# Gelu weights per eight picks instead of sixteen, and the weighted sum five steps behind the dots instead of nine

## The chip, the cores and the metric

One core of a Trainium2 chip runs the whole program. The metric is device time in microseconds (us) of one execution; of several executions the median is taken. The trace comes from one profiled execution of the same program.

## The reference, cut to what matters

A hybrid layer is computed for 1024 prompt rows and 64 sample rows: RMSNorm, a projection, a gated delta rule on 4 heads, a forgetting attention on 8 heads, an output projection, then the expert layer that this change touches, then a gated projection and a final norm. The expert layer, per row `t` with 8 heads of 16 picks (128 picks per row):

```python
e    = i1 * N_KEYS + i2                       # 128 expert numbers per row
gate = softmax(cv)                            # over the 16 picks of a head
a    = einsum('thk,td->thk' over d, take(u_tab, e), x)     # one dot of 1024 per pick
wgt  = gate * gelu(a)
y    = einsum('thk,thkd->td', wgt, take(v_tab, e))         # weighted sum of 128 rows of 1024
```

Gelu and the product with the gate act on each pick alone, so they can be taken for any set of picks whose dots are done.

## The kernel before, in words

The work is cut into tiles of 128 rows, and `build` writes one **pass** (`body`) after another, with a barrier of all engines between them: pass 0 has only the front part of tile 0 (norms, projections, both mixers, the choice of the picks); passes 1 to 7 run the front of tile i together with the expert layer of tile i-1 (from pass 2 on also the tail of tile i-2); the sample pass runs the front of the 64 sample rows with the expert layer of tile 7; the folded pass has the expert layer of the sample rows (64 picks for 128 half-rows) and a tail; the last has only a tail.

Inside a pass the order is a list of **slots** (`PLAN`, written by `make_plan`). Each slot names parts of the front and tail; every engine walks through the slots in order and does its share of these parts. After the parts of a slot come the expert steps of the slot (`Schedule`): two u steps (gather 128 rows of `peer_u`, 512 KB, and one dot per row on VectorE, line 1409) and two v steps (gather 128 rows of `peer_v` and add them, weighted, to the sum). A v step is done either on VectorE (line 1417, `scalar_tensor_tensor`) or on TensorE (line 1011, with a 128x128 diagonal matrix that ScalarE makes of the weights, line 731); `on_tensor` decides it by the slot.

The v steps of a slot belong to picks whose u steps stood `LAG` = 9 slots earlier. So slots 0 to 8 have u steps only, slots 9 to 63 both, slots 64 to 72 v steps only; 73 slots in all. When the 16 picks of a head have their dots (8 slots), ScalarE takes their gelu at the start of slot 8, 16, ... (line 736, after the diagonals of that slot and ahead of the slot's parts) and VectorE multiplies it with the gate (line 1401, behind the slot's parts); the signals are `w_gelu` and `w_ready`.

All gathers are issued by GpSimd (line 486) in the order of the steps into a ring of 8 buffers: gather n waits until step n-8 has been used (`consumed`). The first three u gathers of a pass (`AHEAD`) are issued at the end of the pass before, when the new expert numbers are there (`gate_done`, set by the last of the six `pick_gate` parts, in slot 68, lines 1375 and 1378); that pass waits for their landing. GpSimd also does one product of `pick_gate` (line 505) in slot 67, in its own order between the gathers. The weights of the projections come in pieces of 1 MB through a ring of 3 buffers on SyncE's queue (line 264).

Of the kernel before, what the change touches and what calls it, by code (L numbers as in the profile page):

```python
# [8 lines left out]
ACT = mybir.ActivationFunctionType  # L9
# [18 lines left out]
HP, KEYS, TOP = 8, 128, 16  # L28
EXPERTS = KEYS * KEYS
PICKS = HP * TOP  # L30
# [8 lines left out]
AHEAD = 3  # L39
DIAGS = 4  # L40
PER_SLOT = 2
HEAD_SLOTS = TOP // PER_SLOT
LAG = HEAD_SLOTS + 1


TAIL_PIECES = {f"gate{j}": ("gate", 256 * j, 256) for j in range(4)}
# [26 lines left out]
def on_tensor(k):  # L73

    slot = k // PER_SLOT + LAG
    if 23 <= slot < 43:
# [8 lines left out]
class Schedule:  # L85

    def __init__(self, picks, on_tensor):
        self.picks = picks
        self.slots = picks // PER_SLOT + LAG
        self.order = []  # L90
        for s in range(self.slots):
            own = []
            for j in range(PER_SLOT):
                if s < self.slots - LAG:
                    own.append(("u", PER_SLOT * s + j))
                if s >= LAG:
                    own.append(("v", PER_SLOT * (s - LAG) + j))
            self.order.append(own)
# [12 lines left out]
def build(nc, t, out):  # L111
    ctx = ExitStack()
    with ctx:
        def sb(name, shape, dt=F32):
            return ctx.enter_context(nc.sbuf_tensor(name, shape, dt))
# [109 lines left out]
        dots = sb("dots", [P, PICKS])  # L225
        wgt = sb("wgt", [P, PICKS])
# [8 lines left out]
        S = dict(zip(names, sems))  # L235
# [126 lines left out]
        def body(front=None, peer=None, tail=None, blocks=TILES, plan=None,  # L362
# [33 lines left out]
            def wait_landed(eng, n):  # L396

                before = 1 if n % RING < AHEAD else 0
                if n >= AHEAD:
                    eng.wait_ge(landed[n % RING], 16 * (n // RING + 1 - before))  # L400

            def wait_used(eng, kind, k):

                n = sched.number[kind, k]
                eng.wait_ge(consumed[n % RING], n // RING + 1)
# [14 lines left out]
            with nc.Block() as block:  # L420
# [117 lines left out]
                def _(act):  # L538
# [184 lines left out]
                    for s in range(len(plan)):  # L723
                        if peer:
                            for k in [k for kind, k in sched.order[s] if kind == "v" and k in sched.tensor]:

                                m = sched.tensor[k]
                                act.wait_ge(S["w_ready"], k // TOP + 1)
                                if m >= DIAGS:
                                    wait_used(act, "v", sched.tensor_picks[m - DIAGS])  # L730
                                act.activation(diag[0:peer, m % DIAGS, 0:peer], ident[0:peer, 0:peer], ACT.Copy,  # L731
                                               scale=wgt[0:peer, k:k + 1]).then_inc(S["diag_ready"], 1)
                            if s and s % HEAD_SLOTS == 0 and s // HEAD_SLOTS <= sched.picks // TOP:
                                h = s // HEAD_SLOTS - 1
                                wait_used(act, "u", TOP * h + TOP - 1)
                                act.activation(wgt[0:peer, TOP * h:TOP * h + TOP],  # L736
                                               dots[0:peer, TOP * h:TOP * h + TOP], ACT.Gelu)\
                                    .then_inc(S["w_gelu"], 1)
                        for name in plan[s]:
                            next_part(name)  # L740
# [285 lines left out]
                def _(v):  # L1026
# [365 lines left out]
                    for s in range(len(plan)):  # L1392
                        for name in plan[s]:
                            next_part(name)
                        if not peer:
                            continue
                        if s and s % HEAD_SLOTS == 0 and s // HEAD_SLOTS <= sched.picks // TOP:
                            h = s // HEAD_SLOTS - 1
                            v.wait_ge(S["w_gelu"], h + 1)
                            c = slice(TOP * h, TOP * h + TOP)  # L1400
                            v.tensor_tensor(wgt[0:peer, c], wgt[0:peer, c], gate_c[0:peer, c], ALU.mult)\
                                .then_inc(S["w_ready"], 1)
                        for kind, k in sched.order[s]:
                            n = sched.number[kind, k]
                            r = n % RING
                            row = ring[0:peer, r, :]
                            if kind == "u":
                                wait_landed(v, n)
                                v.tensor_tensor_reduce(out=row, in0=row, in1=xn_c[0:peer, :], scale=1.0, scalar=0.0,  # L1409
                                                       op0=ALU.mult, op1=ALU.add, accum_out=dots[0:peer, k:k + 1])\  # L1410
                                    .then_inc(consumed[r], 1)
                            elif k not in sched.tensor:
                                wait_landed(v, n)
                                v.wait_ge(S["w_ready"], k // TOP + 1)
                                if last_add is not None:
                                    wait_used(v, *last_add)
                                v.scalar_tensor_tensor(out=h_c[0:peer, :], in0=row, scalar=wgt[0:peer, k:k + 1],  # L1417
                                                       in1=h_c[0:peer, :], op0=ALU.mult, op1=ALU.add)\
                                    .then_inc(consumed[r], 1)
                                last_add = (kind, k)  # L1420
                    if peer:
# [4 lines left out]
                        for g in range(2):  # L1426
                            c = slice(512 * g, 512 * g + 512)
# [57 lines left out]
def make_plan():  # L1485

    plan = [[] for _ in range(FULL.slots)]

    def at(slot, *names):
        plan[slot].extend(names)  # L1490

    def spread(name, *slots):
        for s in slots:
            at(s, name)

    spread("tail_norm", 0, 1, 2)
    spread("norm_mix", 0, 1, 2)
    spread("fox_past", 3, 4, 5)
    for j in range(6):
        at(3 + j, f"conv_in{j}")  # L1500
    for g in range(3):
        spread(f"conv{g}", 5 + 2 * g, 6 + 2 * g, 7 + 2 * g)
    at(9, "ba_g")
    at(10, "fox_v1")
    spread("gates", 11, 12)
    for j in range(4):
        at(11 + j, f"gate{j}")
    spread("gdn", 12, 13, 14, 15, 16)
    at(15, "proj0")
    at(16, "proj0", "proj1", "fox_v0")  # L1510
    at(17, "proj1", "fox_k0")
    spread("tail_fin", 18, 19, 20)
    at(18, "fox_k1")
    at(19, "fox_q0")
    at(20, "fox_q1")
    spread("fox_keys", 20, 21)
    at(21, "g")
    at(22, "silu_g")
    s = 22
    spread("inv0", s, s + 1)  # L1520
    for l in range(1, LEVELS):
        spread(f"inv{l}", s + 2 * l - 1, s + 2 * l, s + 2 * l + 1)
    s += 2 * LEVELS
    spread("state", s, s + 2, s + 3, s + 4, s + 5)
    spread("gdn_norm", s + 6, s + 7)
    start = [21 + (9 * h + 2) // 4 for h in range(HB)] + [99]
    for h in range(HB):
        s = start[h]
        spread(f"fox_s{h}", *([s] if s != start[h - 1] + 2 else []), s + 1)
        at(s + 2, f"fox_o{h}")  # L1530
        if start[h + 1] == s + 2:
            at(s + 2, f"fox_s{h + 1}")
        spread(f"fox_o{h}", s + 2, s + 3)
    spread("fox_norm", s + 5, s + 6)
    spread("mix_turn", s + 7, s + 8)
    s += 9
    for j in range(4):
        spread(f"out{j}", s + (2 * j) // 3, s + (2 * j) // 3 + 1)
    s += 3
    spread("norm_ffn", s, s + 1, s + 2, s + 3)  # L1540
    s += 3
    for j in range(HP):
        at(s + j, f"wq{j}")
        if j % 2:
            at(s + j, f"scores{j // 2}")
            at(s + j + 1, f"halves{j - 1}")
            at(s + j + 2, f"halves{j}")
            at(s + j + 3, f"pairs{j // 2}")
    s += HP + 3
    spread("pick_gate", s, s + 1, s + 2, s + 3, s + 4, s + 5)  # L1550
    at(HP * HEAD_SLOTS + 1, "hand_rows")
    assert s + 5 < FULL.slots, s
    return plan


PLAN = make_plan()
FIRST_PLAN = first_plan()

# [35 lines left out]
```

## Time and profile before

| what | value |
|---|---|
| median of 3 runs | 4310.57 us (4282.62 to 4318.11) |
| the profiled execution | 4289.45 us |
| its span, first to last instruction | 4287.7 us |
| outside the span | 1.75 us |
| VectorE busy | 3298.2 us (77%) |
| GpSimd busy | 2583.1 us (60%) |
| TensorE matmul busy | 2891.3 us (67%) |
| ScalarE busy | 813.3 us (19%) |
| gathers (GpSimd's queue) | 1140.99 MB of 1454.12 MB |

Busy times are averages over stages with different limits: inside a pass the DMA engines, GpSimd's issuing and VectorE take turns. Passes 1 to 7 and the sample pass take about 450 to 510 us each, the folded pass 204 us. A window below is a stretch of the span in us; DMA share is the mean busy share of the 16 DMA engines (it can read slightly above 1), GB/s what they moved.

### The profile page before, as it was taken

To read this page: it belongs to the slowest core of one execution; us is meant where nothing else is said; L and a number is where in the kernel's file an instruction comes from. 1 tells how busy PE (TensorE), PEld (TensorE's weight loads), DVE (VectorE), ACT (ScalarE), POOL (GpSimd) and SP (SyncE) were. 2 spreads that over 40 slices of the span, in tenths; PEclk is the share of its full clock that TensorE was granted. 3 is DMA by queue.
4 is the path that set the end of the run, shared out by engine and by line. 5 is a ranking of instruction groups with operands and counts; after the bars stand their busy time and mean duration, and the time that the engine had idled before them with its cause. 6 is when DMAs were issued, how large, how long until landed. Compare 5 with 4: busy or idle time off the path is not lost. (4 is left out here: it accounts for less than half of the span.)

```text
span 4287.7 us, 39164 instructions
## 1 busy us (share of the span) xinstructions
PE 2891.3 (67%) x12714; PEld 1950.3 (45%) x12714; DVE 3298.2 (77%) x6492; ACT 813.3 (19%) x1609; POOL 2583.1 (60%) x2285
## 2 busy tenths in 40 slices
PE   6747665865777666867677577776688565766456
PEld 5634443543455344544355345544455334535122
DVE  3477978787977888697878897788868785787764
ACT  2112111211122112221122112211222112211111
POOL 0037766576656756576656666675666654675674
PEclk9868788987889788988799788988798787868677
DMA  5259998999899998999899989999898989999896
GB/s 185 93 223 372 356 385 303 413 357 370 338 375 370 356 382 317 397 360 379 305 412 355 364 337 370 374 342 392 314 405 309 365 320 277 386 349 362 275 387 238
DMA packets 388058, 1454.12 MB, mean 339 GB/s; under 512 B 64528, under 2 KB 67536, under 8 KB 353296
## 3 DMA queue, kind: packets, MB, share of 16 engines
q0 software_dynamic: 313344, 1140.99, 71.3%
q1 hardware_dynamic: 73200, 305.92, 18.4%
q10 hardware_dynamic: 1312, 4.72, 0.3%
q8 instruction: 103, 1.69, 0.2%
q14 instruction: 99, 0.81, 0.1%
HBM read 1441.69 MB, written 9.51 MB: 338 GB/s over the span
## 5 line engine op out<-in xcount | busy, mean ns | idle before, releaser
L486 POOL DMA_INDIRECT ring<-peer_u,idx_c x1061 | 1267.6, 1195 | 782.4 <-DVE dots L1409 402.5
L1011 PE MATMUL bank<-ring,diag 128*128 128x512 f32 x1920 | 1176.6, 750 | 796.9 <-DMA ring<-peer_v,idx_c 715.6
L1409 DVE CUSTOM_DVE_ANT_0 ring<-ring,xn_c 128x1024 f32<-128x1024 f32 x1088 | 1314.7, 1224 | 441.4 <-DMA ring<-peer_u,idx_c 403.4
L486 POOL DMA_INDIRECT ring<-peer_v,idx_c x1088 | 1204.1, 1107 | 619.9 <-issue 268.6
L1011 PEld LDWEIGHTS bank<-ring,diag 128*128 128x128 f32 x1920 | 411.8, 233 | 1335.8 <-DMA ring<-peer_v,idx_c 901.0
L1417 DVE SCALAR_TENSOR_TENSOR h_c<-ring,wgt,h_c 128x1024 f32<-128x1024 f32 x608 | 785.8, 1292 | 213.3 <-DMA ring<-peer_v,idx_c 203.4
L775 PEld LDWEIGHTS bank<-aT,wring 128*128 128x128 f32 x4608 | 567.4, 203 | 118.2 <-issue 41.0
L775 PE MATMUL bank<-aT,wring 128*128 128x128 f32 x4608 | 573.3, 287 | 64.8 <-DVE aT L1049 27.0
L779 PE MATMUL bank<-wring,aT 128*128 128x256 f32 (+1 forms) x1440 | 342.2, 395 | 36.4 <-DVEq L1071 22.2
L779 PEld LDWEIGHTS bank<-wring,aT 128*128 128x128 f32 x1440 | 282.8, 199 | 111.8 <-issue 62.7
L731 ACT ACTIVATE diag<-ident,wgt 128x128 f32<-128x128 f32 x480 | 179.1, 393 | 361.9 <-PE bank L1011 278.0
L505 POOL TENSOR_TENSOR arena<-arena 128x256 f32<-128x256 f32 x72 | 67.8, 970 | 218.7 <-DVE arena L1340 218.5
L779 PE MATMUL bank<-wring,arena 128*128 128x256 f32 (+2 forms) x648 | 169.7, 415 | 0.8 <-DVE arena L1049 0.8
L552 ACT ACTIVATE arena<-bank 128x256 f32<-128x256 f32 (+1 forms) x108 | 41.5, 384 | 608.7 <-PE bank L775 463.2
L779 PEld LDWEIGHTS bank<-wring,arena 128*128 128x128 f32 (+1 forms) x648 | 124.1, 193 | 52.2 <-issue 33.5
L857 PE MATMUL bank<-arena 128*128 128x128 f32 x432 | 75.3, 328 | 91.2 <-DVE arena L1177 71.8
L674 ACT ACTIVATE arena<-bank 128x512 f32<-128x512 f32 (+3 forms) x104 | 50.2, 483 | 373.6 <-PE bank L943 373.6
L666 ACT ACTIVATE arena<-arena,fneg 128x256 f32<-128x256 f32 (+7 forms) x72 | 53.7, 746 | 331.5 <-DVE fneg L1263 331.4
L857 PEld LDWEIGHTS bank<-arena 128*128 128x128 f32 x432 | 64.4, 228 | 114.5 <-DVE arena L1177 84.7
L932 PE MATMUL bank<-kTc,fqT 128*128 128x512 f32 (+3 forms) x208 | 91.9, 525 | 11.4 <-DVE arena L1243 11.4
L736 ACT ACTIVATE wgt<-dots 128x16 f32<-128x16 f32 x68 | 14.7, 216 | 444.4 <-DVE dots L1409 444.2
L1304 DVE MAX8 arena<-arena 128x8 f32<-128x128 f32 (+1 forms) x216 | 61.9, 328 | 46.1 <-ACT arena L698 43.8
(264 smaller groups left out, 3078.2 us busy)
## 6 DMA issues: line engine op xcount, KB each, us to landing
wring<-piece_wq SPq DMA_DIRECT2D x72, 1024.0 KB, 8.4
wring<-piece_conv_in SPq DMA_DIRECT2D x54, 1024.0 KB, 8.5
wring<-piece_out SPq DMA_DIRECT2D x36, 1024.0 KB, 8.0
wring<-piece_gate SPq DMA_DIRECT2D x36, 1024.0 KB, 8.2
wring<-piece_fox_k SPq DMA_DIRECT2D x18, 1024.0 KB, 7.9
wring<-piece_fox_q SPq DMA_DIRECT2D x18, 1024.0 KB, 8.0
ring<-peer_v,idx_c POOLq DMA_INDIRECT x1088, 6.6
ring<-peer_u,idx_c POOLq DMA_INDIRECT x1061, 7.1
```

The lines of the kernel that those rows point to most:

```text
L486: pool.indirect_dma_start(out=ring[0:rows, n % RING, :], out_offset=None, in_=t["peer_" + kind], in_offset=bass.IndirectOffsetOnAxis(ap=id ...
L505: last = pool.tensor_tensor(e3, e3, over(sif[:, 2 * h + 1, :], TOP), ALU.mult)
L666: act.activation(pbuf[h % 2][:, 0:keys], pbuf[h % 2][:, 0:keys], ACT.Exp, bias=fneg[:, h:h + 1], accum_out=fsum[:, h:h + 1]).then_inc(S["p ...
L731: act.activation(diag[0:peer, m % DIAGS, 0:peer], ident[0:peer, 0:peer], ACT.Copy, scale=wgt[0:peer, k:k + 1]).then_inc(S["diag_ready"], 1)
L775: last = pe.matmul(b[:, m * P:m * P + rows], wt[:, k, m * P:(m + 1) * P], actT[:, k, 0:rows], start=(k == 0), stop=(k == DK - 1))
L779: last = pe.matmul(b[0:rows, 0:w], actT[:, k, 0:rows], wt[:, k, :], start=(k == 0), stop=(k == k8 - 1))
L857: last = pe.matmul(AB[0][:, h * P:(h + 1) * P], mt[:, h, :], tinv[:, h, :], start=True, stop=True)
L932: pe.matmul(SB[g][:, 0:w], fqT[:, h, :], kTc[:, h // 2, c], start=True, stop=False)
L1011: last = pe.matmul(YB[g][0:peer, :], diag[0:peer, m % DIAGS, 0:peer], ring[0:peer, r, 512 * g:512 * g + 512], start=(m == 0), stop=(m == l ...
L1304: last = v.max(vals[:, 0:8], values)
L1409: v.tensor_tensor_reduce(out=row, in0=row, in1=xn_c[0:peer, :], scale=1.0, scalar=0.0, op0=ALU.mult, op1=ALU.add, accum_out=dots[0:peer, k ...
L1417: v.scalar_tensor_tensor(out=h_c[0:peer, :], in0=row, scalar=wgt[0:peer, k:k + 1], in1=h_c[0:peer, :], op0=ALU.mult, op1=ALU.add)\
```

## The change

A group is now half a head, 8 picks, which are complete after 4 slots. ScalarE takes a gelu of 8 columns at the start of slots 4, 8, 12, ... 64, VectorE multiplies 8 columns, and the lag is 5 slots. A pass with 128 picks has 69 slots instead of 73, the folded pass 37 instead of 41. The parts of front and tail stay in their slots, and `on_tensor` decides by the slot as before: 56 of 128 picks on TensorE.

```diff
-HEAD_SLOTS = TOP // PER_SLOT
-LAG = HEAD_SLOTS + 1
+GROUP = TOP // 2
+GROUP_SLOTS = GROUP // PER_SLOT
+LAG = GROUP_SLOTS + 1
...
-                                act.wait_ge(S["w_ready"], k // TOP + 1)
+                                act.wait_ge(S["w_ready"], k // GROUP + 1)
...
-                            if s and s % HEAD_SLOTS == 0 and s // HEAD_SLOTS <= sched.picks // TOP:
-                                h = s // HEAD_SLOTS - 1
-                                wait_used(act, "u", TOP * h + TOP - 1)
-                                act.activation(wgt[0:peer, TOP * h:TOP * h + TOP],
-                                               dots[0:peer, TOP * h:TOP * h + TOP], ACT.Gelu)\
+                            if s and s % GROUP_SLOTS == 0 and s // GROUP_SLOTS <= sched.picks // GROUP:
+                                g = s // GROUP_SLOTS - 1
+                                wait_used(act, "u", GROUP * g + GROUP - 1)
+                                act.activation(wgt[0:peer, GROUP * g:GROUP * g + GROUP],
+                                               dots[0:peer, GROUP * g:GROUP * g + GROUP], ACT.Gelu)\
                                     .then_inc(S["w_gelu"], 1)
...
-                            v.wait_ge(S["w_gelu"], h + 1)
-                            c = slice(TOP * h, TOP * h + TOP)
+                            v.wait_ge(S["w_gelu"], g + 1)
+                            c = slice(GROUP * g, GROUP * g + GROUP)
...
-    at(HP * HEAD_SLOTS + 1, "hand_rows")
+    at(PICKS // PER_SLOT + 1, "hand_rows")
```

On GpSimd, the start of pass 1 before. `peer_u` gathers feed dots, `peer_v` gathers the weighted sum; `idx_c` holds the expert numbers of this pass. Three u gathers were issued at the end of pass 0, so 19 u gathers stand ahead of the first v:

```order
L486 DMA ring<-peer_u,idx_c 128x1024 x16
L486 DMA ring<-peer_v,idx_c 128x1024
L486 DMA ring<-peer_u,idx_c 128x1024
L486 DMA ring<-peer_v,idx_c 128x1024
L486 DMA ring<-peer_u,idx_c 128x1024
```

The same place after the change (its line numbers are one higher):

```order
L487 DMA ring<-peer_u,idx_c 128x1024 x8
L487 DMA ring<-peer_v,idx_c 128x1024
L487 DMA ring<-peer_u,idx_c 128x1024
L487 DMA ring<-peer_v,idx_c 128x1024
L487 DMA ring<-peer_u,idx_c 128x1024
```

Eight u gathers fewer stand ahead of the first v: the four slots 5 to 8 now have two v gathers each.

On GpSimd, the end of pass 1 before: the last v gathers, the product of `pick_gate`, and the three gathers for the next pass with the new numbers `idx_n`:

```order
L486 DMA ring<-peer_v,idx_c 128x1024 x7
L505 TENSOR_TENSOR arena<-arena 128x256 x8
L486 DMA ring<-peer_v,idx_c 128x1024 x12
L486 DMA ring<-peer_u,idx_n 128x1024 x3
L420 UNCONDITIONAL_BRANCH
```

After:

```order
L487 DMA ring<-peer_v,idx_c 128x1024 x7
L506 TENSOR_TENSOR arena<-arena 128x256 x8
L487 DMA ring<-peer_v,idx_c 128x1024 x4
L487 DMA ring<-peer_u,idx_n 128x1024 x3
L421 UNCONDITIONAL_BRANCH
```

The eight v gathers of slots 69 to 72 no longer stand between the product and the three gathers for the next pass.

On ScalarE, in pass 1 after the change, slots 26 to 29: the gelu of slot 28 (line 737) stands between an exp and a copy of the attention (lines 667 and 675) where no gelu stood, with a table load for itself and one for the exp behind it:

```order
L732 ACTIVATE diag<-ident,wgt 128x128 [waits consumed3,w_ready]
L667 ACTIVATE arena,fsum<-arena,fneg 128x256 [waits s_max]
L737 ACT_TABLE_LOAD
L737 ACTIVATE wgt<-dots 128x8 [waits consumed4]
L675 ACTIVATE arena<-bank6 128x256 [waits p_tr,o_fox]
L732 ACTIVATE diag<-ident,wgt 128x128 [waits consumed7,w_ready]
L667 ACT_TABLE_LOAD
L667 ACTIVATE arena,fsum<-arena,fneg 128x256 [waits s_max]
```

Over the whole program ScalarE has 136 gelus instead of 68 and 281 table loads instead of 217.

## Rows read from the trace of the kernel before

**Rows 1.** The page: span, and busy time of each engine.

```profile
span 4287.7 us, 39164 instructions
PE 2891.3 (67%) x12714; PEld 1950.3 (45%) x12714; DVE 3298.2 (77%) x6492; ACT 813.3 (19%) x1609; POOL 2583.1 (60%) x2285
```

**Rows 2.** Windows of pass 4: us, busy time per engine, PEclk, DMA share, GB/s.

```profile
1655.00:1680.00 25.00, 16.78 (x114) 15.64 (x114) 19.29 (x34) 4.94 (x9) 19.08 (x15) 0.75 0.85 291
1680.00:1800.00 120.00, 97.29 (x440) 71.16 (x441) 85.00 (x140) 35.05 (x66) 67.11 (x58) 0.90 1.02 411
1840.00:1930.00 90.00, 59.06 (x281) 40.19 (x282) 85.83 (x147) 20.80 (x42) 69.20 (x64) 0.87 0.98 370
2088.00:2103.00 15.00, 9.24 (x16) 3.58 (x16) 14.76 (x20) 3.43 (x8) 12.89 (x12) 0.80 0.55 178
```

**Rows 3.** Windows 25 to 145 us into passes 2, 7 and the sample pass.

```profile
749.90:869.90 120.00, 98.07 (x446) 70.40 (x445) 86.90 (x143) 35.90 (x66) 68.48 (x58) 0.91 1.02 414
...
3080.80:3200.80 120.00, 96.67 (x448) 70.86 (x447) 86.56 (x141) 35.89 (x66) 68.31 (x58) 0.91 1.02 411
...
3561.10:3681.10 120.00, 82.86 (x399) 64.75 (x400) 76.62 (x132) 29.92 (x55) 58.72 (x48) 0.83 0.93 345
```

**Rows 4.** DMA queues from 1680 to 1800: packets, MB, share of 16 engines.

```profile
q0 software_dynamic: 8449, 30.77, 64.1%
q1 hardware_dynamic: 2600, 17.93, 36.4%
```

**Rows 5.** Timeline of the end of pass 3: start, us, engine, instruction, idle before.

```profile
1638.26 0.29 DVE L1378 TENSOR_TENSOR gate_n<-gate_n,st 128x128 f32<-128x128 f32 x1
...
1645.11 1.59 POOL L486 DMA_INDIRECT ring<-peer_u,idx_n  x1 [0.30 <-issue]
...
1648.24 1.02 POOL L486 DMA_INDIRECT ring<-peer_u,idx_n  x1 [0.31 <-PE bank L1011]
...
1655.99 0.33 SPq L424 DMA_DIRECT2D arena<-p_prompt  x1
```

**Rows 6.** Timeline of the end of pass 0, which has no expert steps.

```profile
258.90 0.29 DVE L1378 TENSOR_TENSOR gate_n<-gate_n,st 128x128 f32<-128x128 f32 x1
...
262.16 0.94 POOL L486 DMA_INDIRECT ring<-peer_u,idx_n  x1 [0.30 <-issue]
...
268.93 0.33 SPq L426 DMA_DIRECT2D x<-x_prompt  x1
```

**Rows 7.** Timeline of the end of the sample pass, the last of eight such ends.

```profile
4030.82 0.29 DVE L1375 TENSOR_TENSOR gate_n<-gate_n,st 128x128 f32<-128x128 f32 x1
...
4048.47 0.33 SPq L424 DMA_DIRECT2D arena<-p_prompt  x1
```

**Rows 8.** Lines 1401 and 736: durations min/median/max in ns; VectorE's idle time before 1401.

```profile
L1401 DVE TENSOR_TENSOR wgt<-wgt,gate_c x68: 159/175/579, 308.4 to 4220.6; 128x16 f32<-128x16 f32 x68
  ACT wgt L736: 5.8, 13
L736 ACT ACTIVATE wgt<-dots x68: 215/215/217, 308.2 to 4219.4; 128x16 f32<-128x16 f32 x68
L736 ACT ACT_TABLE_LOAD  x67: 1283/1283/1283, 306.3 to 4158.1; - x67
```

**Rows 9.** Timeline of ScalarE in pass 4: gelu of slot 8, then the exp behind slot 24's.

```profile
1694.98 0.22 ACT L736 ACTIVATE wgt<-dots 128x16 f32<-128x16 f32 x1 [0.57 <-DVE dots L1409]
...
1817.29 1.28 ACT L666 ACT_TABLE_LOAD   x1
...
1818.58 0.83 ACT L666 ACTIVATE arena<-arena,fneg 128x640 f32<-128x640 f32 x1
```

**Rows 10.** The page: the v step on VectorE.

```profile
L1417 DVE SCALAR_TENSOR_TENSOR h_c<-ring,wgt,h_c 128x1024 f32<-128x1024 f32 x608 | 785.8, 1292 | 213.3 <-DMA ring<-peer_v,idx_c 203.4
```

**Rows 11.** Windows of the folded pass: u steps only, then both kinds.

```profile
4060.00:4070.00 10.00, 0.00 (x0) 0.00 (x0) 7.61 (x13) 0.00 (x0) 8.41 (x6) 0.50 0.87 306
...
4180.00:4190.00 10.00, 5.40 (x7) 2.00 (x8) 6.28 (x11) 0.73 (x2) 7.87 (x8) 0.65 0.97 363
```

More of the change, by code:

```diff
@@ L1396, in _ @@
                             continue
-                        if s and s % HEAD_SLOTS == 0 and s // HEAD_SLOTS <= sched.picks // TOP:
-                            h = s // HEAD_SLOTS - 1
-                            v.wait_ge(S["w_gelu"], h + 1)
-                            c = slice(TOP * h, TOP * h + TOP)
+                        if s and s % GROUP_SLOTS == 0 and s // GROUP_SLOTS <= sched.picks // GROUP:
+                            g = s // GROUP_SLOTS - 1
+                            v.wait_ge(S["w_gelu"], g + 1)
+                            c = slice(GROUP * g, GROUP * g + GROUP)
                             v.tensor_tensor(wgt[0:peer, c], wgt[0:peer, c], gate_c[0:peer, c], ALU.mult)\
@@ L1413, in _ @@
                                 wait_landed(v, n)
-                                v.wait_ge(S["w_ready"], k // TOP + 1)
+                                v.wait_ge(S["w_ready"], k // GROUP + 1)
                                 if last_add is not None:
```

## The prediction

> **What bounds the kernel now.** I read the page first: no engine is busy all the time [rows 1], so the bound changes from stage to stage and the windows of one pass come next. They show four stages [rows 2]. In the first 25 us of pass 4 the DMA engines move 291 GB/s; GpSimd issues gathers for 19.1 of these 25 us, and 15 gaps of 0.3 us between them fill most of the rest. In the next 120 us the DMA share is 1.02 at 411 GB/s while VectorE, TensorE and GpSimd all have gaps: the DMA engines are the bound there. Passes 2 to 7 all show this stage, at 411 to 414 GB/s (the first and the last are shown) [rows 3]; the queues explain it, gathers and weight pieces together take 64.1% + 36.4% of the engines [rows 4]. From 1840 to 1930 VectorE is busy 85.8 of 90 us and GpSimd issues without a pause (69.2 us, and 64 gaps of 0.3 us): both are full. From 2088 to 2103, where the picks of the next tile are finished (slots 65 to 68), VectorE is busy 14.8 of 15 us and the DMA engines only 0.55.
>
> The last place to read is the end of a pass. `gate_done` comes with line 1378 at 1638.26; but GpSimd still has v gathers of slots 69 to 72 to issue, its three gathers for the next pass start at 1645.11, the last at 1648.24, and the next pass starts at 1655.99 [rows 5]: 17.73 us after line 1378. The eight such ends take 17.0 to 18.2 us, 17.6 on average; the last one is 4048.47 - 4030.82 = 17.65 [rows 7].
>
> **The change, part by part.** No gather and no v step disappears. Per pass with 128 picks, eight v steps (8 gathers, 4 diagonals and TensorE products, 4 line-1417 steps) leave slots 69 to 72 and the same number comes into slots 5 to 8. The rest of the order keeps its slots. So the sum has three terms per pass: what slots 5 to 8 pay, what the end saves, what the additional gelus cost.
>
> *Slots 5 to 8.* They end where the gelu of slot 8 stands, at 1694.98 in pass 4 [rows 9], 39 us into the pass, so their transfers fall into the start of the DMA-bound stage [rows 2]. Eight gathers are 8 x 524,288 B = 4.19 MB; at 412 GB/s this is 10.2 us, and since the weights and the gathers of the following slots stand in the same saturated stage, nothing after it gives that back. Before the stage, GpSimd's issuing limits the gathers, and it would issue the same number there. The least that the step can cost is VectorE's part alone: 4 x 1.29 = 5.2 us [rows 10], if the transfers found holes. A cost below zero is excluded, the work is added there. For the six passes 2 to 7 I take 10.2. Pass 1 has no tail pieces and the sample pass moves 345 GB/s in the same stage [rows 3], so both have holes; I take the middle, 7.7. Together 6 x 10.2 + 2 x 7.7 = 77 us, between 41 and 82.
>
> The rule that speaks against the change is in the Trainium skill, "Trainium Kernel Development and Optimization", Key Constraints: DMAs issued from SyncE, ScalarE and GpSimd run on the same 16 engines and interleave; here the shares of the two queues sum to 100.5%, so the trace agrees [rows 4]. In "DMA: Bandwidth & Descriptors", Anatomy of one DMA, the variable part of a transfer is bytes / 436e9 s, which gives 1.20 us per gather; by that estimate this term would be some 6% smaller, about 72 us.
>
> *The end.* The gathers for the next pass are then ready to go right behind `gate_done`, since GpSimd has four v gathers fewer than eight left there: 4 after its product instead of 12. What remains is what pass 0 shows, which has nothing else queued: line 1378 at 258.90, third gather at 262.16, next pass at 268.93, so 10.03 us [rows 6]. The saving is 17.6 - 10.0 = 7.6 us, times 8 passes = 61 us. It is hidden by nothing: the barrier waits for these gathers. What is late next is VectorE's tail (one 1.29 us step, two adds, two copies) and its landing in ScalarE; these end about 5 us after line 1378, before the gathers land. Bounds: 5 us if the last v steps hold VectorE and then the barrier longer, 8.6 if `gate_done` itself comes a microsecond earlier with less issuing beside it.
>
> *The gelus.* There are 8 more per pass. VectorE pays 0.175 us for the product and so far waited 5.8 us over 68 gelus, 0.085 each [rows 8]: 0.26 us. Those of slots 4, 12 and 20 fall in stages that the DMA engines or GpSimd bound and are covered; if that cover went, they would add 0.8 us per pass. The five others (28, 36, 44, 52, 60) lie where VectorE is full: 1.3 us per pass. On ScalarE a gelu between exps needs two table loads and itself: 1.28 + 0.22 + 1.28 = 2.8 us [rows 8, 9]; this is ahead of the exp of the attention in slots 28 and 36. Queued behind it on ScalarE are the exp, the copies of the transposed scores and the diagonals; TensorE waits for these. ScalarE is busy 20.8 of 90 us there [rows 2], so I take 0.3 us for each of the two. Bounds: 0 if all is hidden, 2 x 2.8 + 1.3 = 6.9 us per pass if both delays go through. I take 1.9 us per pass, 15 us in all, between 0 and 55.
>
> "ScalarE: Activation LUTs", What ACT_TABLE_LOAD costs, in the Trainium skill counts 2.66 us for a switch, the load and a drain of 1380 ns. The trace shows the load alone: the exp starts 0.01 us behind its load's end [rows 9]. By the page's figure the two slots would delay by 5.5 us each and the upper bound would be 12.3 us per pass.
>
> *The folded pass.* Eight u gathers leave the stretch with u steps only, at 306 GB/s or 1.71 us each, for the mixed stretch at 363 GB/s or 1.44 us [rows 11]: 8 x 0.27 = 2.2 us saved; four more gelus cost 1. I take -1.
>
> *The sum.* 77 - 61 + 15 - 1 = +30 us. Against the profiled execution: its span 4287.7 and 1.75 us around it, 4289.45, becomes 4319. The median of the runs shown is 21 us above the profiled execution; the same 30 us on it give 4340.6 us, +0.7%.
>
> **The rivals.**
>
> *The moved v steps fit into holes (faster).* Place: slots 5 to 8. If the saturated stage is saturated only because pieces and gathers are asked for early, the eight gathers cost 0 to 5.2 us instead of 10.2. For it: VectorE idles 35 of 120 us in that stage, and the first 25 us run at 291 GB/s. Against it: the stage lasts 120 us at a full DMA share in every one of six passes, and landings are what VectorE waits for at the v steps (203 us over the program) [rows 10]. The point of decision is 7.6 - 1.9 = 5.7 us per pass: below it the change is faster. At 0 it gives 8 x (1.9 - 7.6) - 1 = -47 us, so 4264; at 5.2, -5 us, 4306.
>
> *The additional gelus hold the engines together (slower).* ScalarE may run ahead of VectorE for only four slots instead of eight. If each of the five gelus in the VectorE-bound stages cost its whole chain (two loads, gelu, product, 3.0 us), the gelus cost 15 us per pass, 120 in all, and the sum is 77 - 61 + 120 - 1 = +135, 4446. For it: the gelu's wait is in ScalarE's order ahead of the parts. Against it: so far VectorE waited only 13 times of 68 [rows 8].
>
> *The end saves little (slower).* If the end keeps 14 of its 17.6 us because the last v steps, the sum over both accumulators and ScalarE's copy follow behind `gate_done`, the saving is 3.6 us, 29 in all, and the sum is +62, 4373. Against it: VectorE's part behind line 1378 adds up to 5 us.
>
> **How the numbers follow.** A measurement of this kernel can tell about 1%, 43 us, from no change. My forecast (+5 to +60 us) has a chance of 0.52, of which 0.12 lie above 43 us. Holes: 0.20, half of it beyond -43. Gelus: 0.15, nearly all beyond +43. The end: 0.13, likewise. This gives faster 0.10, within 1% 0.55, slower 0.35. For the range I take 41 to 82 for the first term, 40 to 69 for the second, 0 to 55 for the third, not all at their ends at once: -26 to +79 us, or 4285 to 4390.
>
> **What would show it right or wrong.** In the changed profile the time from line 1379 (1378 before) to the next pass should be about 10 us instead of 17.6. The DMA-bound stage should start at the same 25 us and be about 10 us longer at the same 411 GB/s; if it keeps its length, the first term is wrong and the time falls. The windows where VectorE is full should be 1 to 3 us longer per pass; if VectorE's idle time in front of line 1402 grows from 5.8 us to more than 40, the second rival holds. If passes 2 to 7 change by less than 1 us each, the two large terms cancel more exactly than I think.

## The result and the profile after

The changed kernel takes 4313.26 us (median of 20 runs, 4303.81 to 4331.03). The kernel before, run beside it, takes 4294.97 us (median of 20, 4282.62 to 4318.11). The ratio is 1.0040, 95% interval 1.0028 to 1.0053: slower by 0.4%, some 18 us. The forecast was 4340.6 us. Of the 27 us between, 15.6 come from the base (the median of three runs on which it stood was that much above the median of 20) and 12 from the terms (30 forecast, 18 measured).

The page of the changed kernel, the lines that answer to [rows 1] and to the gelu in [rows 8]:

```profile
span 4313.8 us, 39364 instructions
PE 2904.1 (67%) x12714; PEld 1964.1 (46%) x12714; DVE 3301.0 (77%) x6560; ACT 903.9 (21%) x1741; POOL 2563.9 (59%) x2285
...
L732 ACT ACTIVATE diag<-ident,wgt 128x128 f32<-128x128 f32 x480 | 177.4, 392 | 220.1 <-DVE wgt L1402 148.6
...
L737 ACT ACTIVATE wgt<-dots 128x8 f32<-128x8 f32 x136 | 28.3, 208 | 635.4 <-DVE dots L1410 635.0
...
L737 ACT ACT_TABLE_LOAD x107 | 137.3, 1283 | 1.9
```

ScalarE is 90.6 us busier, and VectorE 2.8 us; the span of the profiled execution is 26.1 us longer. A busy time that grows says nothing yet on where the span grew. 6.3 of the 26.1 us are pass 0, which has the same instructions in both kernels and in the other profiled executions lay between 1.4 us less and 5.5 us more than before: that is how executions differ.

The end of pass 3, the place of [rows 5]:

```profile
1664.10 0.29 DVE L1379 TENSOR_TENSOR gate_n<-gate_n,st 128x128 f32<-128x128 f32 x1
1664.31 2.69 DVE L1418 SCALAR_TENSOR_TENSOR h_c<-ring,wgt,h_c 128x1024 f32<-128x1024 f32 x2
1664.66 1.74 POOL L487 DMA_INDIRECT ring<-peer_u,idx_n  x1 [5.27 <-DVE gate_n L1379]
1666.70 1.11 POOL L487 DMA_INDIRECT ring<-peer_u,idx_n  x1 [0.30 <-issue]
...
1668.12 0.94 POOL L487 DMA_INDIRECT ring<-peer_u,idx_n  x1 [0.30 <-issue]
...
1674.72 0.33 SPq L425 DMA_DIRECT2D arena<-p_prompt  x1
```

From line 1379 to the next pass it is now 1674.72 - 1664.10 = 10.62 us, where [rows 5] show 17.73. GpSimd now waits 5.27 us for `gate_done` instead of having v gathers left to issue.

The stages of pass 4, shifted by the passes' starts (1674.72 against 1655.99) and, in the last two rows, by some 9 us more, the delay of this pass; they answer to [rows 2]:

```profile
1674.00:1699.00 25.00, 17.04 (x112) 15.84 (x113) 18.38 (x34) 6.72 (x12) 18.17 (x15) 0.67 0.86 302
1699.00:1819.00 120.00, 95.55 (x438) 68.09 (x437) 84.10 (x134) 37.18 (x69) 69.43 (x62) 0.94 1.01 407
1868.00:1958.00 90.00, 58.95 (x280) 38.85 (x281) 85.16 (x148) 24.55 (x45) 70.21 (x64) 0.84 0.98 367
2116.80:2131.80 15.00, 10.08 (x15) 3.92 (x16) 14.76 (x20) 2.22 (x5) 9.20 (x9) 0.73 0.44 147
```

In the first three rows a window of fixed length reads nearly alike in both kernels: it shows what a stage is, not how long it lasts. So I took marks: the start of a pass is its load of `p_prompt`, as in [rows 5], and the product behind the gelu (line 1401 before, 1402 after) marks slots 8, 16 and so on. In pass 5 the mark of slot 8 lies 41.70 us behind the start before and 50.50 after, that of slot 16 another 56.00 and 58.90. The kernel before, from start to slot 8 and on to slot 16, columns as in [rows 2]:

```profile
2120.00:2161.70 41.70, 30.71 (x219) 29.09 (x220) 33.73 (x59) 10.23 (x18) 25.40 (x20) 0.78 0.94 351
2161.70:2217.70 56.00, 45.05 (x178) 29.80 (x177) 44.83 (x75) 19.30 (x36) 36.82 (x32) 0.97 1.02 409
```

After:

```profile
2142.31:2192.81 50.50, 38.06 (x235) 31.66 (x236) 37.63 (x63) 13.06 (x24) 30.31 (x25) 0.81 0.96 358
2192.81:2251.71 58.90, 46.63 (x179) 31.61 (x177) 46.59 (x78) 21.92 (x38) 39.17 (x35) 0.91 1.01 406
```

41.70 x 351 GB/s are 14.6 MB, 50.50 x 358 are 18.1 MB: 8.8 us and 3.4 MB more in this pass. Over passes 2 to 7 the mean is 40.2 us and 13.91 MB before, 49.7 us and 17.97 MB after: 9.5 us for 4.06 MB, which is 427 GB/s.

All marks against the profiled execution of before, us, mean over passes 1 to 7 and the sample pass (plus: later; "gate" is line 1378/1379):

| kernel | slot 8 | slot 16 | slot 64 | gate | pass | folded pass | ratio |
|---|---|---|---|---|---|---|---|
| the change | 9.3 | 10.7 | 9.5 | 9.4 | 2.7 | -2.5 | 1.0040 |
| groups of 8, lag 9 | 0.8 | 0.1 | 0.8 | 0.9 | 0.8 | -4.0 | 0.9984 |
| groups of 4, lag 3 | 12.6 | 15.2 | 15.7 | 15.8 | 8.0 | -3.1 | 1.0136 |
| late v steps in the gate slots | 0.7 | 0.1 | -2.4 | -1.1 | 1.9 | -5.1 | 1.0049 |
| change, slots 5-8 on TensorE | 5.7 | 10.4 | 9.8 | 9.8 | 3.1 | -3.8 | 1.0055 |
| change, few rows in slots 5-8 | 5.2 | 7.4 | 7.3 | 7.1 | 0.4 | -0.4 | 1.0003 |
| change, both of these | 2.9 | 6.7 | 6.5 | 6.3 | -0.4 | -1.3 | 1.0009 |
| change, gate pieces cut | 8.6 | 5.4 | 4.4 | 4.4 | -2.2 | -9.4 | 0.9947 |
| before, gate pieces cut | 0.1 | -3.4 | -2.8 | -2.8 | -2.7 | -18.1 | 0.9921 |
| before, product on GpSimd in slots 5-8 | 3.5 | 2.6 | 2.7 | 2.4 | 2.6 | -8.6 | 1.0049 |
| extra v steps in slots 53-60 | 0.2 | -0.1 | 6.7 | 6.7 | -0.1 | -6.7 | 1.0010 |
| extra v steps in slots 44-51 | 0.2 | -1.1 | 9.1 | 9.1 | 2.4 | -2.7 | 1.0018 |

Single passes of one kernel scatter by some 4 us around these means, and the folded pass by more (-5.1 and -8.6 in the two kernels where it has the instructions of before); the ratios rest on many runs each. The row of the change reads: a pass loses 9.3 us by slot 8, keeps that to the gate, and gets 6.7 back at its end. 8 x 2.7 - 2.5 = +19 us, and the ratio gives +18.

### The profile page after: what moved, and what is told of

It is laid out like the page before. It is cut to its first block and busy times, and to the rows that moved or that the text cites. A ratio compares the mean times of both kernels' runs of the same rounds, so it can differ in the third digit from the quotient of the medians.

```text
span 4313.8 us, 39364 instructions
## 1 busy us (share of the span) xinstructions
PE 2904.1 (67%) x12714; PEld 1964.1 (46%) x12714; DVE 3301.0 (77%) x6560; ACT 903.9 (21%) x1741; POOL 2563.9 (59%) x2285
## 5 line engine op out<-in xcount | busy, mean ns | idle before, releaser
L487 POOL DMA_INDIRECT ring<-peer_u,idx_c x1061 | 1242.3, 1171 | 779.2 <-DVE dots L1410 404.3
L780 PE MATMUL bank<-wring,aT 128*128 128x256 f32 (+1 forms) x1440 | 351.9, 403 | 44.7 <-DVEq L1072 29.5
L732 ACT ACTIVATE diag<-ident,wgt 128x128 f32<-128x128 f32 x480 | 177.4, 392 | 220.1 <-DVE wgt L1402 148.6
L737 ACT ACTIVATE wgt<-dots 128x8 f32<-128x8 f32 x136 | 28.3, 208 | 635.4 <-DVE dots L1410 635.0
L737 ACT ACT_TABLE_LOAD x107 | 137.3, 1283 | 1.9
```

Of the source, the lines that this page charges most:

```text
L487: pool.indirect_dma_start(out=ring[0:rows, n % RING, :], out_offset=None, in_=t["peer_" + kind], in_offset=bass.IndirectOffsetOnAxis(ap=id ...
L737: act.activation(wgt[0:peer, GROUP * g:GROUP * g + GROUP], dots[0:peer, GROUP * g:GROUP * g + GROUP], ACT.Gelu)\
L780: last = pe.matmul(b[0:rows, 0:w], actT[:, k, 0:rows], wt[:, k, :], start=(k == 0), stop=(k == k8 - 1))
```

## The experiments

Each was timed beside the kernel before; a ratio stands with its 95% interval.

**Groups of 8 alone.** The gelus of the change, with the lag of before:

```diff
-LAG = GROUP_SLOTS + 1
+LAG = TOP // PER_SLOT + 1
```

> Groups of 8 picks as in the change, but the lag stays at 9 steps, so only the additional gelus (64 + 4) are left of the change. My theory from the changed trace (the delay of a pass stays at about 9.5 us from slot 8 to slot 64): the additional gelus cost nothing that shows, ratio to before 1.000, at most +5 us. The prediction's term: +15 us, ratio 1.0035. The rival that the gelus hold the engines together: all of the +18 us of the change or more, ratio 1.004 and up. The marks inside a pass (gelu of slots 8 to 64) should stay within 2 us of before by my theory, and drift apart with each new gelu by the rival.

Measured: 4297.04 us against 4301.8, ratio 0.9984 (0.9965 to 1.0003). No mark moves beyond the scatter. Its page has the same gelus and table loads as the change:

```profile
L737 ACT ACTIVATE wgt<-dots 128x8 f32<-128x8 f32 x136 | 28.3, 208 | 633.2 <-DVE dots L1410 632.6
...
L737 ACT ACT_TABLE_LOAD x107 | 137.3, 1283 | 1.9
```

So the 68 additional gelus and 64 additional table loads cost at most 1 us by the interval. Before the gelus ScalarE waits for dots (633 us in all): it has time to spare.

**Lag 3, groups of 4.** The same step taken further; the slots stay as in the change:

```diff
-GROUP = TOP // 2
+GROUP = TOP // 4
```

> Groups of 4 picks and a lag of 3 steps: four more v steps per pass move to slots 3 and 4; slots 67 and 68 have none. My theory: the start of a pass pays about 5 us more than the change (4 gathers at 1.2 to 1.28 us), the end cannot fall below the 11 us from the last gate product to the next pass because only the three gathers stand there already, so +40 us on the change, about +58 us on before, ratio 1.013. If the order's end still gives something back, ratio 1.004 as the change or below. If the start costs VectorE's part alone (2 steps of 1.29 us), +21 us on the change, ratio 1.009.

Measured: 4360.02 us, ratio 1.0136 (1.0106 to 1.0167). Four more v steps at the start make the mark of slot 16 15.2 us late, and the end, 7.7 us shorter than before (9.95 us instead of 17.63, on average), gives back hardly more than in the change. The two terms scale as they should: the start pays per v step, the end is worth its 7 us once.

**Late v steps in the gate slots.** Before's groups and lag, but the eight v steps of slots 69 to 72 stand in slots 65 to 68, so that the start has nothing to pay. In these slots the first v step is done on VectorE and all others on TensorE:

```diff
+V_AT = [s for s in range(9, 64) for _ in range(2)] + [64] * 2 + [65] * 3 + [66] * 4 + [67] * 4 + [68] * 5
...
-                if s >= LAG:
-                    own.append(("v", PER_SLOT * (s - LAG) + j))
...
+            vs = [("v", k) for k in range(picks) if v_at[k] == s]
```

> The groups of 16 and the lag of the kernel before, slots 0 to 63 unchanged; only the eight v steps of slots 69 to 72 are taken into slots 65 to 68 (3, 4, 4 and 5 v steps there, one of each slot on VectorE, the others on TensorE), so a pass has 69 slots. My theory: the start pays nothing, the DMA engines (busy 0.55 there) take the eight gathers beside VectorE's finishing of the picks, and the time from the last gate product to the next pass is 11 to 13 us instead of 17.6: -5 to -6.7 us per pass, -40 to -53 us in all, ratio 0.988 to 0.991. If GpSimd's or TensorE's order in these slots holds the gate product up by as much as the end saves, ratio 1.000; if the eight gathers are bound by bytes there too, also 1.000.

Measured: 4319.63 us, ratio 1.0049 (1.0026 to 1.0071): a miss. The timeline of the end of its pass 3:

```profile
1632.91 7.12 POOL L517 TENSOR_TENSOR arena<-arena 128x256 f32<-128x256 f32 x8
...
1640.18 0.97 POOL L498 DMA_INDIRECT ring<-peer_v,idx_c  x1 [0.16 <-issue]
...
1644.66 0.29 DVE L1390 TENSOR_TENSOR gate_n<-gate_n,st 128x128 f32<-128x128 f32 x1
...
1651.08 0.94 POOL L498 DMA_INDIRECT ring<-peer_v,idx_c  x1 [0.30 <-issue]
1652.32 0.94 POOL L498 DMA_INDIRECT ring<-peer_u,idx_n  x1 [0.30 <-issue]
...
1661.57 1.28 DVE L1440 TENSOR_TENSOR h<-h_c,bank 128x512 f32<-128x512 f32 x2 [7.99 <-PE bank L1023]
...
1662.89 1.06 ACT L757 ACTIVATE h_c<-x 128x1024 f32<-128x1024 f32 x1 [7.79 <-DVE h L1440]
...
1665.26 0.33 SPq L436 DMA_DIRECT2D arena<-p_prompt  x1
```

Nine v gathers still follow GpSimd's product, one per 1.24 us or slower, so the gathers for the next pass start 7.7 us after line 1390 and the end takes 20.6 us. The start pays nothing, as it should. What ends last here is not the landing of these three gathers (1661.31 for the last) but the v steps: VectorE's addition of TensorE's sum waits 7.99 us for TensorE, until 1661.57, and ScalarE's copy follows. So GpSimd, issuing one gather after another, starts this chain late, and TensorE, which does more of the steps here, ends it. Whether the bytes would have held it up as well is not shown: from line 1390 to the first of the three gathers the DMA share is 0.91 at 306 GB/s.

**The v steps of slots 5 to 8 on TensorE.** In the change, VectorE's share of them (4 x 1.29 us) is taken away:

```diff
+    if slot < 9:
+        return True
     if 23 <= slot < 43:
```

> The change, with all eight v steps of slots 5 to 8 on TensorE (four more there, four fewer on VectorE). The run with few rows left 5 us of the delay at slot 8 standing, which is what four steps of 1.29 us on VectorE make. Theory one: bytes (10 us) and VectorE (5 us) run side by side and the longer decides; then taking VectorE's part away alone changes nothing, delay at slot 8 still 9 to 10 us, ratio 1.004 as the change. Theory two: the two add up (about 5 each); then the delay falls to about 5 us, 4 to 5 us less per pass, ratio 0.995 to 0.997.

Measured: 4326.82 us against 4296.53, ratio 1.0055 (1.0029 to 1.0082). Slot 8 is only 5.7 us late, slot 16 is 10.4 us late, as in the change. In passes 2 to 7 the stretch to slot 16 has 41.8 MB against 37.7 before, as much as in the change, and takes 10.9 us more, where the change takes 11.2. The mark of slot 8 is earlier than in the change while 1.1 MB of weight pieces less have been fetched by then; they follow before slot 16. By slot 16, taking VectorE's share away gains nothing.

**Few rows.** In the change, the v gathers of the first eight picks fetch 32 of 128 rows in the passes with 128 picks (the v steps still read all 128 rows of the buffer, where the other 96 hold older numbers, so the output is not the reference's); alone, and together with the edit above:

```diff
-gather(n, kind, k, peer, idx_c, landed[n % RING])
+few = kind == "v" and k < 8 and sched is FULL
+gather(n, kind, k, 32 if few else peer, idx_c, landed[n % RING])
```

> The change, but the v gathers of picks 0 to 7 fetch 32 of the 128 rows (the other rows of these picks are left out of the sum as they should be); instructions, waits and order stay. It takes 3.1 of the 4.2 MB from slots 5 to 8 of a pass. If the start of a pass is bound by bytes, the delay at the gelu of slot 8 falls from 9.5 us to 2 to 3 us and the time falls by about 7 us per pass, 56 us in all, to ratio 0.991. If it is the work of VectorE (5.2 us) and the order that delays, the delay at slot 8 stays at 5 us or more and the ratio at 1.000 or above.

> Both at once: 32 of 128 rows for the v gathers of picks 0 to 7 (the other rows of these picks are left out of the sum), and all eight v steps of slots 5 to 8 on TensorE. By both theories the delay at slot 8 should fall to 1 to 2.5 us (a quarter of the bytes is left) and a pass be about 5 to 6 us shorter than before, ratio 0.988 to 0.991. If a third cost sits there (the order of the steps: the ring of 8 covers two slots instead of four, or TensorE's queue holding v steps between the projections), 3 us or more of the delay stay.

Measured: ratio 1.0003 (0.9985 to 1.0021) alone, 1.0009 (0.9989 to 1.0028) together. Both miss. Together, a quarter of the moved gathers' bytes stays, yet by slot 16 6.7 of 10.7 us stay, too. Windows of the second kernel's pass 5, to slot 8 and to slot 16:

```profile
2134.86:2176.86 42.00, 34.71 (x204) 27.81 (x205) 34.04 (x59) 13.82 (x27) 29.22 (x25) 0.81 0.94 319
2176.86:2239.86 63.00, 52.61 (x225) 36.29 (x223) 45.47 (x76) 22.31 (x40) 39.38 (x35) 0.97 1.01 401
```

The DMA share to slot 8 is still 0.94, at 319 GB/s instead of 358: by this share alone one would not see that bytes are gone. The eight gathers also cost something that isn't their bytes or VectorE's share. Two further tests were meant to separate this.

**Bytes of the other queue.** Both kernels with the four weight pieces of the tail's gate projection cut to a sixteenth (the other columns keep older weights, so the tail's gate is not the reference's):

```diff
-            sp.dma_start(wring[:, n % WRING, 0:src.shape[1]], src).then_inc(loaded, 16)
+            width = 128 if name.startswith("gate") else src.shape[1]
+            sp.dma_start(wring[:, n % WRING, 0:width], src[:, 0:width]).then_inc(loaded, 16)
```

> The changed kernel, with the four weight pieces of the tail's gate projection cut from 1,024 KB to 64 KB each (128 of their 2,048 columns are fetched, the rest of each buffer keeps older weights; the output of the tail's gate is then not that of the reference). Nothing else moves: the gathers, their order, the ring and GpSimd's issuing stay. That takes 3.93 MB of SyncE's transfers out of the first slots of passes 2 to 7 and of the sample pass, nearly what the moved v gathers add there (4.19 MB). Theory one (the bytes of the stage whose DMA share is full decide): slot 8 comes 9.5 us earlier than in the changed kernel, so at the same time as before, and the seven passes give 7 x 9.3 = 65 us: 4313 - 65 = 4248 us, ratio to before about 0.989. Theory two (what the moved gathers cost is their issuing, or places in the ring of 8 buffers, whatever the bytes beside them): slot 8 stays 7 us or more behind before, and the ratio is 1.000 to 1.004.

> The kernel before with the same cut of the four gate pieces (64 KB instead of 1,024 KB each; the output of the tail's gate is not that of the reference). Theory one (bytes decide): slot 8 comes 9 us earlier than before in passes 2 to 7 and the time is 65 us shorter, ratio 0.985. Theory two (issuing or ring places decide): slot 8 comes less than 3 us earlier, ratio 0.995 to 1.000.

Measured: the change 4269.49 us, ratio 0.9947 (0.9927 to 0.9966); before 4250.84 us against 4289.62, ratio 0.9921 (0.9895 to 0.9946). Both lie between the theories. Three readings help. First, the cut does not fall where I had put it: to slot 8 the bytes are as without it (17.88 MB against 17.97), because SyncE's queue fetches the next piece instead, and slot 8 stays 8.6 us late. Second, from slot 8 to slot 16 the bytes fall by 3.9 and 4.2 MB and the time by only 5.1 and 3.5 us, where 412 GB/s would give 9.6 and 10.3. Pass 5 of the cut change, slots 8 to 16:

```profile
2177.87:2232.07 54.20, 46.98 (x177) 33.16 (x176) 46.44 (x79) 21.91 (x38) 36.34 (x33) 0.87 0.96 365
```

The share is below full now. What the engines waited for in this stretch (releaser: total us, times, longest):

```profile
POOL ring L488 <- DVE dots L1411: 9.4, 4, 5.2
POOL ring L488 <- issue: 8.8, 29, 0.3
...
DVE ring L1411 <- DMA ring<-peer_u,idx_c: 6.0, 4, 2.6
```

and in the same stretch of the change with whole pieces:

```profile
DVE ring L1410 <- DMA ring<-peer_u,idx_c: 10.4, 7, 3.2
...
POOL ring L487 <- issue: 8.8, 29, 0.3
...
POOL ring L487 <- DVE dots L1410: 6.8, 3, 3.2
```

VectorE waits 4.4 us less for landings and GpSimd 2.6 us more for ring places that VectorE frees. VectorE is now busy 46.4 of 54.2 us, where it was 46.6 of 58.9, but it still waits 6.0 us for landings, so it is not yet the only limit; which limit comes next is not shown. Third, since both cuts leave the stretch to slot 8 as it was, the pair says nothing on the start itself: there the change loses 8.6 - 0.1 = 8.5 us with the cut as without it.

**A product on GpSimd.** Meant to test GpSimd's time alone: before, with a product of 128x352 numbers that nobody reads behind each u gather of slots 5 to 8:

```diff
+if sched is FULL and kind == "u" and 10 <= k < 18:
+    spend(pool.tensor_tensor(scr[:], xn_c[:, 0:352], xn_c[:, 352:704], ALU.mult))
```

> The kernel before (groups of 16, lag 9, nothing moved) with one product of 128x352 numbers on GpSimd behind each of the eight u gathers of slots 5 to 8, into a buffer that nothing reads: about as much of GpSimd's time as one gather takes to issue (some 1.2 us each, 10 us per pass), but no transfer, no place in the ring and no work for VectorE. Theory one (the transfers' bytes make the 9.3 us that the moved v steps cost by slot 8): slot 8 comes less than 2 us later than before, the time is 4295 to 4310, ratio 1.000 to 1.003. Theory two (GpSimd's issuing makes them): slot 8 comes 6 to 10 us later in all eight passes and nothing gives it back, 4345 to 4375, ratio 1.012 to 1.018.

```profile
L523 POOL TENSOR_TENSOR scr<-xn_c 128x352 f32<-128x352 f32 x64 | 65.2, 1018 | 1.3
```

Measured: 4317.28 us against 4299.36, ratio 1.0049 (1.0031 to 1.0067). 8 x 1.02 = 8.1 us of GpSimd per pass make slot 8 3.5 us late, without a byte. But it is not GpSimd's time alone that changes. The page has VectorE 44.3 us busier than before (3342.5 against 3298.2 us) with the same 6492 instructions:

```profile
PE 2890.1 (67%) x12714; PEld 1960.5 (46%) x12714; DVE 3342.5 (78%) x6492; ACT 812.1 (19%) x1609; POOL 2667.2 (62%) x2349
```

In pass 5 one operation of VectorE takes 1.61 us where a product runs on GpSimd beside it, and 0.69 us where none does:

```profile
2159.51 1.61 DVE L1097 TENSOR_TENSOR cT<-cT,arena 128x512 f32<-128x512 f32 x1
2159.62 0.94 POOL L523 TENSOR_TENSOR scr<-xn_c 128x352 f32<-128x352 f32 x1
...
2173.45 0.69 DVE L1097 TENSOR_TENSOR cT<-cT,arena 128x512 f32<-128x512 f32 x1
```

The 0.92 us more are about the length of the product. Gathers show nothing of the kind: in pass 5 of the change, with two gathers more per slot, the same operation takes 0.69 us. So this test slowed VectorE by 5.5 us per pass and doesn't tell what GpSimd's time costs.

What VectorE did up to the marks tells more of all these kernels. Means of passes 2 to 7 from the traces, in us and MB, the other rows as differences to the first; "landings" is VectorE's idle time that ended with the landing of a gather:

| kernel | slot 8 | busy | landings | slot 16 | busy | landings | MB by slot 16 |
|---|---|---|---|---|---|---|---|
| before | 40.2 | 33.7 | 0.0 | 98.2 | 79.0 | 11.5 | 37.7 |
| the change | +9.5 | +3.8 | +6.0 | +11.2 | +5.0 | +6.5 | +4.1 |
| slots 5-8 on TensorE | +6.1 | +0.3 | +5.0 | +10.9 | +0.3 | +9.8 | +4.1 |
| few rows | +5.1 | +3.8 | +1.8 | +7.5 | +5.0 | +3.0 | +1.0 |
| both of these | +3.0 | +0.2 | +3.2 | +7.1 | +0.3 | +7.0 | +0.9 |
| product on GpSimd | +4.0 | +6.0 | 0.0 | +3.8 | +5.7 | -0.3 | 0.0 |

Four things can be read from it. Before, VectorE waits for no landing up to slot 8; its longest wait in pass 5 is for ScalarE (first line), where the change waits for landings (second line):

```profile
DVE cT L1089 <- ACT zT L552: 2.5, 1, 2.5
DVE ring L1410 <- DMA ring<-peer_u,idx_c: 6.7, 2, 4.2
```

In the change its delay at slot 8 is about the sum of two parts, 3.8 us of its own added work and 6.0 us of landings that come late. When its own part is taken away, the waits for landings grow by nearly as much by slot 16, with all rows and with few. And taking 3.1 of the 4.1 MB away takes off 3.7 us of 11: the larger part stays with the eight additional gathers although most of their bytes are gone. The weight pieces gave back only about half or less of their bytes' time, too, so this test does not fix the bytes' share.

**Another place for the eight v steps.** Groups of 8, first v step in slot 9, and a third v step, on TensorE, in eight later slots:

```diff
+EXTRA = range(53, 53 + 8)
+V_AT = [s for s in range(9, 69) for _ in range(3 if s in EXTRA else 2)]
```

> A placement that should beat both: groups of 8, first v step in slot 9 as before, last in slot 68 as in the change; the eight v steps in question go as a third v step, on TensorE, into slots 53 to 60, where VectorE is the bound and GpSimd and TensorE have gaps. My theory: the start pays nothing (delay at slot 8 below 2 us), the end is 11 us as in the change, and of slots 53 to 60 at most a few us are lost, as the DMA engines move 370 GB/s there against 411 in the saturated stage: -3 to -6.7 us per pass, ratio 0.988 to 0.995. If the bytes or GpSimd's issuing bound these slots as well (10 us for eight gathers), ratio 1.004 as the change.

> The same with the eight additional v steps in slots 44 to 51, where the out projection and the norm leave VectorE, TensorE and GpSimd gaps (51.8, 41.4 and 48 of 70 us busy in pass 4) at 362 GB/s. My theory: as above, -3 to -6.7 us per pass, ratio 0.988 to 0.995; if the landings of the gathers bound this stage, 1.000 to 1.004.

Measured: 4300.36 us, ratio 1.0010 (0.9990 to 1.0030), and 4307.66 us, 1.0018 (0.9996 to 1.0040). The start is free, but slots 53 to 64 pay 6.5 us, slots 44 to 56 some 9, and the end gives 6.7 back. No version here that computes the reference's output beats the kernel before beyond its interval.

## Why the prediction came out as it did

*The stage of slots 5 to 8* (10.2 us for six passes, 7.7 for pass 1 and the sample pass, 77 in all) measured 9.3 x 8 = 75. The single passes are 9.8 (pass 1), 8.4 to 11.1 and 7.3 (sample), so pass 1 paid in full although I gave it holes. The size was right, the reason at best in part. I let bytes hide VectorE's part (10.2 us against 5.2); up to slot 8 the delay is a sum, 3.8 us of VectorE's work and 6.0 us of late landings. I put these slots into the DMA-bound stage, but up to slot 8 VectorE waited for no landing before and was busy 33.7 of 40.2 us. And most of the delay by slot 16 stays when three quarters of the added bytes are gone. That the term came out within 2 us is luck.

"Nothing after it gives that back" held: slot 64 is 9.5 us late. In "Trainium Kernel Development and Optimization", Key Constraints, the Trainium skill says that DMAs issued from SyncE, ScalarE and GpSimd run on the same 16 DMA engines. That fits the shares of the two queues [rows 4], but it does not say that the stage gives time back when bytes go: 3.9 and 4.2 MB less between slots 8 and 16 brought 5.1 and 3.5 us.

*The end* (17.6 - 10.0 = 7.6 us, 61 in all) measured 9.4 - 2.7 = 6.7 us, 53 in all. The eight ends now take 10.5 to 11.3 us, 10.9 on average. The mechanism is as described: in passes 1 to 7 VectorE is done 4.5 us and ScalarE 5.3 us behind line 1379, and the last of the three gathers lands 9.1 to 9.6 us behind it. Pass 0 was 0.9 us too good a model: beside VectorE's last steps the first two gathers now take 1.74 and 1.11 us, where pass 0 shows 1.13 and 0.95. With lag 3, where no v step is left there, the end takes 9.95 us.

*The gelus* ("I take 1.9 us per pass, 15 us in all") are the step that failed among the terms. Groups of 8 alone give a ratio of 0.9984 (0.9965 to 1.0003), so 1 us at most instead of 15, and in the change the delay does not grow between slot 8 (9.3 us) and slot 64 (9.5). In the change VectorE waits more ahead of the product, 28.1 us in 14 cases instead of 5.8 in 13, below the 40 that I had set as the mark of the second rival. Line 1402 of the changed kernel, and who waited:

```profile
L1402 DVE TENSOR_TENSOR wgt<-wgt,gate_c x136: 149/166/570, 294.2 to 4256.8; 128x8 f32<-128x8 f32 x136
its engine sat idle before it (us, times) until:
  ACT wgt L737: 28.1, 14
who waited for it (us, times):
  ACT diag L732: 148.6, 48
```

ScalarE's diagonals wait 148.6 us for the new weights, where they waited 68.8 before, and still the stretch from slot 24 to slot 56 takes 211.5 us instead of 213.3 in passes 2 to 7. Of the 1.9 us, 0.6 were a delay in ScalarE's order, priced as if TensorE stood behind it; ScalarE is 21% busy, and its waits were off the path. The other 1.3 were VectorE's products and their waits in slots where I took VectorE as full; they do not show either, and why is not tested. "ScalarE: Activation LUTs", What ACT_TABLE_LOAD costs, in the Trainium skill, would make a switch dearer still (2.66 us); the loads here last 1283 ns and 64 more of them changed nothing.

*The folded pass* (-1) measured -2.5, inside its scatter.

*The sum* by the measured terms is 75 - 53 + 0 - 2.5 = +19 us where I had 77 - 61 + 15 - 1 = +30. The gelus made my sum 15 us too slow and the end 8 us too fast; that these two errors cancel in part is luck. The other two terms differ by 2 us or less.

*The base* ("the same 30 us on it give 4340.6") is the second step that failed, by 15.6 us, more than all terms together. I put the terms on the median of three runs, although the profiled execution, 21 us below it, was known. Of 20 runs the median was 4294.97, nearer to the profiled 4289.45: against it 4340.6 reads as +46 us, and +18 came.

*The rivals.* Holes: fell, the start pays more than 8 us in seven of eight passes. Gelus hold the engines together: fell. The end saves little: fell, it saved 6.7 of 7.6. The last sign that I named, that passes 2 to 7 change by less than 1 us each because the two large terms cancel, came in three of the six: 8.2, 0.6, 3.6, 0.9, 0.8 and 1.3 us.

*What stays open.* What the eight additional gathers cost at the start beyond their bytes. With few rows and TensorE, slot 16 is 7.1 us late in passes 2 to 7; 0.9 MB more than before make 2 us of that at 412 GB/s. The rest, some 5 us, may be GpSimd's time for them (8 x 1.24 us), the order, in which a v gather now stands between two u gathers, or the ring's 8 places, now shared by four steps per slot. GpSimd is not issuing all the time: up to slot 16 it waits 20.5 us for places in that kernel, and 23.0 us before. No run separates these; a longer ring needs other memory.

## What to carry to other kernels

Work that is moved out of a tail where one engine issues alone is paid for where it arrives: find the stage that takes it, look at what the consuming engine waits for there, and don't price the work by bytes alone. A test that removes bytes from a stage with a full DMA share can give back much less than bytes over rate: here 5.1 and 3.5 us of some 10. A test that loads one engine has to be read on all the others too: the product on GpSimd slowed VectorE. Extra waits on an engine with much idle time cost nothing here; before pricing such a wait, ask who stands behind it. And a forecast of half a percent needs a base of more than three runs.

## What was unexpected of the hardware

In these runs the DMA share is no measure of throughput: with v gathers of 32 instead of 128 rows (and their steps on TensorE) the stretch to slot 8 reads 0.94 at 319 GB/s, and before 0.94 at 351. A product on GpSimd can hold up VectorE for its whole length: 0.69 us become 1.61 beside a product of 0.94. And a gather's 0.94 us and 0.30 us gap on GpSimd (1.24 us) are so near to its 524,288 B at 412 GB/s (1.27 us) that the sum comes out alike by either cause. With a quarter of the bytes the larger part of the delay stayed, so the bytes alone do not explain it.
